# VectorE's top-16 search of a later PEER group in steps between the dot products of the present one

## The reference

```python
s = jnp.einsum('thsd,hsnd->thsn', q, sub_keys)
s1, i1 = lax.top_k(s[:, :, 0], PEER_TOPK)
s2, i2 = lax.top_k(s[:, :, 1], PEER_TOPK)
cand_s = s1[..., :, None] + s2[..., None, :]        # 16 x 16 candidates
cand_i = i1[..., :, None] * PEER_N_KEYS + i2[..., None, :]
top_s, pos = lax.top_k(cand_s, PEER_TOPK)
idx = jnp.take_along_axis(cand_i, pos, axis=-1)
gate = jax.nn.softmax(top_s, axis=-1)
act = jax.nn.gelu(jnp.einsum('thkd,td->thk', u_emb[idx], xc))
out = jnp.einsum('thk,thkd->td', gate * act, v_emb[idx])
```

## Time and profile before

| | |
|---|---|
| runs | 2319.68, 2320.46, 2325.69 us (median 2320.46) |
| the profiled execution, span | 2319.7 us |
| busy: TensorE | 1812.7 us (78%) |
| busy: VectorE | 1451.5 us (63%) |
| busy: GpSimd | 1186.4 us (51%) |
| busy: ScalarE | 557.3 us (24%) |
| mean granted TensorE clock | 0.917 |
| bytes moved by DMA | 603.01 MB, of it 537.99 MB by the software queue |

### The profile page before, as it was taken

The page is one execution under the profiler, slowest core; times in us unless marked ns, Lnnn a source line. Parts: engine busy times, 40 slices in busy tenths (PEclk is TensorE's granted clock), DMA queues, the critical chain, the costliest instruction groups (busy, mean ns, idle before and its releaser), DMA issues.

```text
span 2319.7 us, 23103 instructions
## 1 busy us (share of the span) xinstructions
PE 1812.7 (78%) x5927; PEld 979.2 (42%) x5927; DVE 1451.5 (63%) x2986; ACT 557.3 (24%) x1159; POOL 1186.4 (51%) x1175
## 2 busy tenths in 40 slices
PE   6778899999997828778777677767866977777677
PEld 6446435779975714333233223223322322333233
DVE  4597674443435378677666775676666766676664
ACT  2223443222332212122112211121211211121121
POOL 6970000000001065777676676765766767677774
PEclk9888899999999969999899998988998989899899
DMA  4301401334421098999998998998999899899997
GB/s 111 64 9 19 100 18 42 91 91 146 144 73 37 19 373 311 374 390 376 370 383 308 385 377 320 390 365 319 395 373 383 329 373 376 320 372 387 389 392 302
DMA packets 239397, 603.01 MB, mean 260 GB/s; under 512 B 38533, under 2 KB 105274, under 8 KB 239290
## 3 DMA queue, kind: packets, MB, share of 16 engines
q0 software_dynamic: 147840, 537.99, 60.3%
q1 hardware_dynamic: 91450, 63.85, 10.0%
HBM read 597.56 MB, written 2.10 MB: 259 GB/s over the span
## 4 chain that ended last, share of the span: by engine, by line
issue 18%; PE 15%; DMA 12%; DVE 11%; POOL 5%; DVEq 1%; ACT 1%; POOLq 0%; ACTq 0%
PE bank L1744 15%; DMA WS<-in_peer_u,R 8%; POOL R L1874 3%; DMA slabs<-in_peer_u,R 3%; POOL WS L1874 2%; DVE R L1326 1%; DVE R L1329 1%; DVE R L1327 1%; DMA R<-in_peer_v,R 1%; DVE R L1373 1%; DVE R L1328 1%; DVE R L1325 1%; POOL slabs L1874 1%; DVE H L1387 1%; DVE R L1347 0%
## 5 line engine op out<-in xcount | busy, mean ns | idle before, releaser
L1744 PE MATMUL bank<-R 128*128 128x512 f32 x2048 | 987.2, 630 | 341.1 <-ACT R L884 220.8
L1744 PEld LDWEIGHTS bank<-R 128*128 128x128 f32 x2048 | 390.4, 199 | 928.5 <-issue 673.6
L1874 POOL DMA_INDIRECT R<-in_peer_v,R x512 | 533.1, 1041 | 157.0 <-issue 142.3
L1373 DVE CUSTOM_DVE_ANT_0 R<-WS,XN 128x1024 f32<-128x1024 f32 x256 | 313.6, 1225 | 183.5 <-DMA WS<-in_peer_u,R 178.9
L1874 POOL DMA_INDIRECT slabs<-in_peer_u,R x256 | 255.8, 999 | 304.1 <-DVEq L1362 97.8
L1373 DVE CUSTOM_DVE_ANT_0 R<-slabs,XN 128x1024 f32<-128x1024 f32 x256 | 313.8, 1226 | 119.4 <-DMA slabs<-in_peer_u,R 103.3
L1874 POOL DMA_INDIRECT WS<-in_peer_u,R x256 | 252.2, 985 | 78.0 <-issue 74.3
L1869 POOL TENSOR_TENSOR FTr<-slabs,FTr 128x2048 fp32r<-128x2048 f32 x1 | 4.5, 4498 | 533.2 <-ACT FTr L626 533.2
L884 ACT ACTIVATE R<-cst,R 128x128 f32<-128x128 f32 x512 | 180.5, 394 | 355.5 <-PE bank L1744 354.5
L1471 PE MATMUL bank<-R 128*128 128x64 f32 (+5 forms) x596 | 186.5, 455 | 45.3 <-ACT R L682 20.2
L1471 PEld LDWEIGHTS bank<-R 128*128 128x128 f32 (+3 forms) x596 | 88.1, 179 | 116.5 <-issue 72.2
(11 more groups left out here) (210 smaller groups left out, 1901.8 us busy)
## 6 DMA issues: line engine op xcount, KB each, us to landing
slabs<-in_w_in SPq DMA_DIRECT2D x17, 512.0 KB, 5.3
slabs<-in_w_mem_kv SPq DMA_DIRECT2D x8, 1024.0 KB, 5.5
slabs<-in_w_peer_q SPq DMA_DIRECT2D x8, 1024.0 KB, 14.9
R<-in_peer_v,R POOLq DMA_INDIRECT x512, 6.5
slabs<-in_w_in SPq DMA_DIRECT2D x4, 1024.0 KB, 14.0
slabs<-in_w_ssm_glu SPq DMA_DIRECT2D x16, 256.0 KB, 3.2
slabs<-in_w_out SPq DMA_DIRECT2D x4, 1024.0 KB, 5.3
slabs<-in_w_mem_q SPq DMA_DIRECT2D x4, 1024.0 KB, 5.2
```

The source lines that it names most:

```text
L1373: dve.tensor_tensor_reduce(prod, Ub[s % URING], xn[:, t, :], 1.0, 0.0, ALU.mult, ALU.add, act_row[:, s:s + 1]).then_inc(dots, 1)
L1744: last = pe.matmul(ps[2 * (t % 2) + n][:, :], diag[s % DRING], Vb[s][:, 512 * n:512 * n + 512], start=(s == 0), stop=(s == TOPK - 1))
L1874: pool.indirect_dma_start(out=dst, out_offset=None, in_=table, in_offset=bass.IndirectOffsetOnAxis(ap=ix[:, s:s + 1], axis=0)).then_inc(si ...
```

## The change

`topk` becomes a generator, `topk_steps`, that gives control back after each operation that the next one depends on; `pick16` replaces `top16`. The wait for an operation's completion (`landed`) now stands ahead of the next step and no longer right behind the operation. `dot_products` takes such a generator (`beside`) and runs two of its steps behind each dot product, and what is left of it behind the last one. A dot product waits for the one before it ahead of its own start, and for the last one at the end. In `head` the call of `topk` is gone, and `dot_products` of g + 1 gets the steps of the search of g + 2; `take_sum` of g - 1 now comes first in the iteration. The negated maximum and the two operations behind it are issued together, and `gates_neg` is raised when the first has landed. The search of groups 0 and 1, ahead of the first dot products, runs its steps in a row as before. The other engines' programs are the same. The operations and their number are the same too.

```diff
@@ -1320,14 +1320,6 @@
                 if apart:
                     dve.sem_inc(apart_dve, 1)
 
-            def top16(vals, spare, v, ix):
-
-                lstep(dve.max(v[:, 0:8], vals), apart=True)
-                lstep(dve.max_index(ix[:, 0:8], v[:, 0:8], vals), apart=True)
-                lstep(dve.match_replace(spare, v[:, 0:8], vals, NEG), apart=True)
-                lstep(dve.max(v[:, 8:16], spare), apart=True)
-                lstep(dve.max_index(ix[:, 8:16], v[:, 8:16], spare), apart=True)
-
             def scores(h, first=False):
 
                 for s in range(2):
@@ -1338,41 +1330,99 @@
                           apart=True)
                 dve.sem_inc(s_copied, 1)
 
+            def lag(ins):
+
+                count[0] += 1
+                ins.then_inc(c_loop, 1)
+                return count[0]
+
+            def landed(n):
+                dve.wait_ge(c_loop, count[1] + n)
+
+            def pick16(vals, spare, v, ix):
+
+                for half in range(2):
+                    src = spare if half else vals
+                    lo = slice(8 * half, 8 * half + 8)
+                    dve.sem_inc(apart_dve, 1)
+                    n = lag(dve.max(v[:, lo], src))
+                    yield
+                    landed(n)
+                    dve.sem_inc(apart_dve, 1)
+                    n = lag(dve.max_index(ix[:, lo], v[:, lo], src))
+                    yield
+                    landed(n)
+                    if not half:
+                        dve.sem_inc(apart_dve, 1)
+                        n = lag(dve.match_replace(spare, v[:, lo], vals, NEG))
+                        yield
+                        landed(n)
+
+            def topk_steps(t):
+
+                for s in range(2):
+                    yield from pick16(SC[:, t, s, :], sc1, tv[:, s, :], ti[:, s, :])
+                lag(dve.tensor_copy(tif, ti))
+                n = lag(dve.tensor_tensor(cand.rearrange("p (a b) -> p a b", a=TOPK),
+                                          tv[:, 0, :].unsqueeze(2).to_broadcast([P, TOPK, TOPK]),
+                                          tv[:, 1, :].unsqueeze(1).to_broadcast([P, TOPK, TOPK]), ALU.add))
+                yield
+                landed(n)
+                yield from pick16(cand, cand1, cv, cpos)
+                n = lag(dve.tensor_scalar(nmx, cv[:, 0:1], -1.0, None, ALU.mult))
+                lag(dve.tensor_scalar(cpp[:, 0:16], cpos, 4, None, ALU.logical_shift_right))
+                m = lag(dve.tensor_scalar(cpp[:, 16:32], cpos, 15, None, ALU.bitwise_and))
+                landed(n)
+                dve.sem_inc(gates_neg, 1)
+                yield
+                landed(m)
+                n = lag(dve.tensor_copy(cpf, cpp))
+                yield
+                landed(n)
+                n = lag(dve.tensor_tensor(eq, iota16.unsqueeze(1).to_broadcast([P, 2 * TOPK, TOPK]),
+                                          cpf.unsqueeze(2).to_broadcast([P, 2 * TOPK, TOPK]), ALU.is_equal))
+                yield
+                landed(n)
+                e4 = eq.rearrange("p (s k) a -> p s k a", s=2)
+                n = lag(dve.tensor_tensor(e4, e4, tif.unsqueeze(2).to_broadcast([P, 2, TOPK, TOPK]), ALU.mult))
+                yield
+                landed(n)
+                n = lag(dve.tensor_reduce(isel, eq, AX.X, ALU.add))
+                yield
+                landed(n)
+                n = lag(dve.scalar_tensor_tensor(idx[t], isel[:, 0:16], float(NK), isel[:, 16:32], ALU.mult, ALU.add))
+                yield
+                landed(n)
+                dve.sem_inc(idx_ready, 1)
+
             def topk(t):
 
-                dve.sem_inc(apart_dve, 1)
-                for s in range(2):
-                    top16(SC[:, t, s, :], sc1, tv[:, s, :], ti[:, s, :])
-                lstep(dve.tensor_copy(tif, ti))
-                lstep(dve.tensor_tensor(cand.rearrange("p (a b) -> p a b", a=TOPK),
-                                        tv[:, 0, :].unsqueeze(2).to_broadcast([P, TOPK, TOPK]),
-                                        tv[:, 1, :].unsqueeze(1).to_broadcast([P, TOPK, TOPK]), ALU.add), apart=True)
-                top16(cand, cand1, cv, cpos)
-                lstep(dve.tensor_scalar(nmx, cv[:, 0:1], -1.0, None, ALU.mult))
-                dve.sem_inc(gates_neg, 1)
-                lstep(dve.tensor_scalar(cpp[:, 0:16], cpos, 4, None, ALU.logical_shift_right))
-                lstep(dve.tensor_scalar(cpp[:, 16:32], cpos, 15, None, ALU.bitwise_and))
-                lstep(dve.tensor_copy(cpf, cpp))
-                lstep(dve.tensor_tensor(eq, iota16.unsqueeze(1).to_broadcast([P, 2 * TOPK, TOPK]),
-                                        cpf.unsqueeze(2).to_broadcast([P, 2 * TOPK, TOPK]), ALU.is_equal))
-                e4 = eq.rearrange("p (s k) a -> p s k a", s=2)
-                lstep(dve.tensor_tensor(e4, e4, tif.unsqueeze(2).to_broadcast([P, 2, TOPK, TOPK]), ALU.mult))
-                lstep(dve.tensor_reduce(isel, eq, AX.X, ALU.add))
-                lstep(dve.scalar_tensor_tensor(idx[t], isel[:, 0:16], float(NK), isel[:, 16:32], ALU.mult, ALU.add))
-                dve.sem_inc(idx_ready, 1)
+                for _ in topk_steps(t):
+                    pass
 
             def gates_of(g, t):
                 dve.wait_ge(gates_exp, g + 1)
                 lstep(dve.reciprocal(rinv, esum))
                 lstep(dve.tensor_scalar(gate[t % 2], ex, rinv, None, ALU.mult))
 
-            def dot_products(g, t):
-
+            def dot_product(g, t, s):
+
+                dve.wait_ge(ld_u[s % URING], (g * 2 + (s // URING + 1)) * 16)
+                if s:
+                    dve.wait_ge(dots, g * TOPK + s)
+                dve.tensor_tensor_reduce(prod, Ub[s % URING], xn[:, t, :], 1.0, 0.0, ALU.mult, ALU.add,
+                                         act_row[:, s:s + 1]).then_inc(dots, 1)
+
+            def dot_products(g, t, beside=()):
+
+                beside = iter(beside)
                 for s in range(TOPK):
-                    dve.wait_ge(ld_u[s % URING], (g * 2 + (s // URING + 1)) * 16)
-                    dve.tensor_tensor_reduce(prod, Ub[s % URING], xn[:, t, :], 1.0, 0.0, ALU.mult, ALU.add,
-                                             act_row[:, s:s + 1]).then_inc(dots, 1)
-                    dve.wait_ge(dots, g * TOPK + (s + 1))
+                    dot_product(g, t, s)
+                    for _ in range(2):
+                        next(beside, None)
+                for _ in beside:
+                    pass
+                dve.wait_ge(dots, (g + 1) * TOPK)
 
             def weights(g, t):
                 dve.wait_ge(gelu_done, g + 1)
@@ -1394,12 +1444,10 @@
                     ahead = not last or t < 2
                     if t == 2 and not last:
                         scores(h + 1)
-                    if ahead:
-                        topk((t + 2) % NT)
                     if not first or t:
                         take_sum(g + (-1), (t - 1) % NT)
                     if not last or t < NT - 1:
-                        dot_products(g + 1, (t + 1) % NT)
+                        dot_products(g + 1, (t + 1) % NT, topk_steps((t + 2) % NT) if ahead else ())
                         weights(g + 1, (t + 1) % NT)
                     if ahead:
                         gates_of(g + 2, t)
```

## The result

The changed kernel took 2420.54 us at the median (2419.41 to 2424.75), the kernel before 2323.07 us beside it: a ratio of 1.0421, 95% interval 1.04 to 1.0442. It is slower by 4.2%, where 7.3% had been forecast. The profiled execution's span is 2417.9 us, against 2319.7.

What follows compares the result with a forecast made beforehand. The kernel before was taken as bounded by row-gather transfers, with holes. Changed: group 2's dots at 916.6 us, 28 periods of 51.95 to 2371.2, then the end at 2488.0; median 2489 us, 7.3% more, range 2440 to 2538.

Steps and rivals of the forecast that it cites:

- The ring: Per group, take_sum, nine dots with 17 search steps, gates_neg, exponential, diagonals, V(g) run serially: 51.95 us against 46.4.
- V(g): TensorE's sum of group g from its diagonals: 30.0 us, bounds 27.7 and 31.
- 17 steps and nine dots: VectorE, from first dot of g + 1 to gates_neg for g + 2: 19.3 us, bounds 17.5 and 21.
- No gaps at all: Low bound of 17 steps and nine dots, with no time lost between operations: 17.5 us.
- Negated maximum to first matmul: From VectorE's search step that raises gates_neg, through ScalarE, to TensorE's first matmul of V(g): 0.85 us.
- take_sum to first dot: VectorE, from take_sum to the next group's first dot product: 1.7 us.
- From the first dot of 30 to the end: From group 30's first dot at 2371.2 us, through the last sums and a tail of 8.9, to 2488.0 us.
- TensorE's clock: TensorE idles over 10 us before every V(g), so each starts slow: 30.0 us and not 27.7.
- rival 3: TensorE stays warm, V(g) takes 27.7 us, the kernel 2422 us; chance 0.05.
- The cover at the loop's top: VectorE's 10.7 us wait for V(g) ahead of take_sum hides the 9.7 us of idle issue there.
- The faster rival: The ring does not close, earlier dots fill the transfers' holes: 41.9 us per group, 2190 us; chance 0.06.
- GpSimd's idle time: GpSimd, which issues the row gathers, idles 12 us of each 52, twice per group; transfers no longer bound.

Runs made afterwards that it cites:

- ScalarE's order and four steps: Changed kernel, but ScalarE makes diagonals of g before exponentials of g + 2, and four search steps stand behind each dot: 2255.74 us, ratio 0.9721.
- The open ring: Changed kernel, but ScalarE makes the diagonals of g before the exponentials of g + 2: 2297.83 us, ratio 0.9908 to the kernel before.

## Why the prediction was right and wrong

**The ring, right.** A closed ring was forecast through take_sum, the dots, gates_neg, the exponentials, the diagonals and V(g), and each of the two joints, cut alone, opened it. Shortening one member moved the time as the sum says.

**The term that failed: 17 steps and nine dots.** It was put at 19.3 us with 17.5 as the low bound and measured 17.0 (1707.09 to 1724.11). The prediction took 1.27 us per dot from the earlier trace rows, where a dot follows a dot that it waits for, and only let a dot fill the gap between two dependent steps. In the changed kernel neither waits for what runs just ahead of it: a step starts 1.15 us behind the dot's start, and the next dot starts before the step has ended. That is 0.12 us behind each of nine dots and 0.12 ahead of eight of them, 2.0 of the 2.3 us by which the term was too large; where the other 0.3 lie was not followed. "No gaps at all" was no lower bound, because operations that do not wait for each other overlap, which the earlier trace rows could not show. The experiment with every wait behind its operation brought the term to 20.5, above the forecast, since a step then starts 1.38 us behind a dot's start. 28 x 2.37 = 66 us separate the forecast first dot of group 30 (2371.2) from the measured one (2301.3), with 3.5 more from the first groups; the whole miss is 68.5. The range's low end, 2440, leaned on the same false bound. (Both low bounds together make 51.95 - 1.8 - 2.3 = 47.85 us and not the 47.65 of the prediction; nothing else hangs on it.)

**The other terms.** V(g) alternates between 29.3 and 30.4 us, mean 29.85, against 30.0. Negated maximum to first matmul 0.83, take_sum to first dot 1.7, both as put. The sum with the measured term is 49.5, measured 49.58. From the first dot of 30 to the end it took 116.6 us, forecast 116.8, but that is two misses that cancel: V(29) ended 47.2 us behind that dot in place of 50.15, and V(30), which waits for its last rows, took 33.2 us and ended 80.3 behind it (forecast 80.2).

**TensorE's clock, right.** The sign that was named, the time from the first matmul to the tenth diagonal (the prediction counts from 0 and calls it diagonal 9), is 5.1 to 6.8 us in every group from 0 to 29, also in those with query products ahead; 3.7 would have been rival 3. The granted clock of the window is 0.83. The measured time, 2420.54, is within 2 us of rival 3's 2422 all the same. That is chance: its 2.3 us per group were looked for in V(g), which kept them, and the steps beside the dots gave up as much. The rule of the Trainium skill ("TensorE: Matmul & The Clock Gate", the two states), by which an idle array falls to 1.2 GHz, holds here: 27.7 us appears only where one V follows another, at the end. In the window with ScalarE's order and four steps the granted clock is 1.00.

**The cover at the loop's top, right.** Before, five passes had 9.7 us of idle issue each. In the changed kernel no such wait of VectorE is left; take_sum waits for TensorE over it. When the ring is open and the cover gone, it is back (waits of VectorE, 1000 to 2300 us, with ScalarE's order changed):

```profile
DVE H L1437 <- issue: 27.1, 5, 5.8
DVE R L1413 <- issue: 7.5, 6, 1.6
```

about 5.4 us per pass ahead of take_sum and 1.5 more ahead of a dot 5 us later. The rule of "Runtime: NRT & Kernel Launch" in the Trainium skill, Instruction fetch mechanics, by which a taken branch out of the resident pages forces a fetch, fits: the idle time stays at the loop's top whatever operation stands there.

**The faster rival, half wrong in its price.** It gave 2190 us for an open ring, by transfers. The open ring gave 2298, because of a cost that no part of the prediction had: gathers stretched beside two-input operations. With gates_neg at 13.3 us the kernel came out at 2316.82, near the point (13.8 us, for the 2320 of the kernel before) that the rival had named.

**GpSimd's idle time, wrong.** It was priced at 0.94 + 0.30 us per gather, though the earlier trace rows already had one of 1.26, and forecast to idle 12 of 52 us, twice per group. It is busy 39.0 us and not 30.1 for the 32 gathers of a group and idles 1.0 us. The ring hid this miss from the time. The transfers ran at 342 GB/s, against 325 forecast.

## What to carry to other kernels

Before work is moved on one engine, list every signal raised within it and who waits for that signal in a fixed order; if the moved work now stands behind something that waits for that waiter, there is a ring, and its period is a plain sum. What opened it here was one order on ScalarE, which had been free before. In that sum, price operations that do not wait for each other by their overlap (here 0.12 us at each side of a 1.2 us operation), not by the spacing of ones that do.

## What the runs showed of the hardware

- A gather's issue on GpSimd takes 0.94 us. One that starts within a VectorE operation with two SBUF inputs ends 0.80 us behind that operation's end, up to 1.99 us in all; operations with one SBUF input don't stretch it. The gather reads its row numbers from SBUF. The Trainium skill ("SBUF — State Buffer", SBUF: two separate sides, the reading of the diagram) says that a two-input operation holds the port pair shared with GpSimd against one that reads SBUF; the stretched gathers agree. It says as much of the other direction, and that no run here shows: dots that start within a gather take 1.20 to 1.23 us in the changed kernel, no more than the others.
- The same kernel took 2323 us on one chip and 2582 us on another. The traces of its variants have 4 KB packets of 159 ns at the median on both.
- Two VectorE operations without a wait between them overlapped by 0.08 us in the records; with a wait, a search step started 0.15 us behind the end of the operation before it.
